# A scaled activation operand rebuilt from the parts of the raw one and a row of token factors, instead of from transposes

## The reference

```
h = rms_norm(x, norm_mix_w)
z = h @ w_in + b_in
```

```
y = xf * lax.rsqrt(jnp.mean(xf * xf, axis=-1, keepdims=True) + EPS)
return (y * g).astype(x.dtype)
```

## Time and profile before

| | |
|---|---|
| median of three runs | 1943.66 us |
| the profiled execution | 1943.68 us |
| its span | 1942.0 us |
| PE busy | 1928.6 us, 99% |
| DVE busy | 1380.6 us, 71% |
| ACT busy | 927.7 us, 48% |
| POOL busy | 237.3 us, 12% |

### The profile page before, as it was taken

How to read it: one execution, slowest core, us unless ns; L and a number is a source line. 1 busy time by engine, 2 the same in 40 slices (tenths; PEclk the granted TensorE clock), 3 DMA queues, 4 the chain that set the end, 5 groups by cost and what they waited for, 6 DMA issues and landing times.

```text
span 1942.0 us, 29945 instructions
## 1 busy us (share of the span) xinstructions
PE 1928.6 (99%) x11950; PEld 1723.7 (89%) x11950; DVE 1380.6 (71%) x1588; ACT 927.7 (48%) x1032; POOL 237.3 (12%) x195
## 2 busy tenths in 40 slices
PE   9999999999999999999999999999999999999998
PEld 7999888889998888888899998888888899998887
DVE  7776766668677666766769677667766769677666
ACT  6564444345645334544554445444544554445443
POOL 0000000000001000000049250000000049250000
PEclk9999999999999999999999999999999999999999
DMA  7544555554356554555444555555555454555553
GB/s 276 195 153 161 188 195 188 183 191 172 131 197 214 186 192 173 195 185 193 163 175 153 174 193 196 182 187 182 202 190 187 166 178 153 173 193 180 183 192 108
DMA packets 50738, 353.37 MB, mean 182 GB/s; under 512 B 6064, under 2 KB 6192, under 8 KB 9040
## 3 DMA queue, kind: packets, MB, share of 16 engines
q1 hardware_dynamic: 47952, 341.93, 50.1%
q0 software_dynamic: 2400, 9.99, 1.6%
q10 hardware_dynamic: 288, 0.05, 0.0%
HBM read 349.85 MB, written 2.10 MB: 181 GB/s over the span
## 4 chain that ended last, share of the span: by engine, by line
PE 90%; DVE 6%; ACT 2%; issue 1%; DMA 0%; DVEq 0%; POOL 0%; POOLq 0%; SPq 0%; ACTq 0%
PE ps L226 19%; PE ps L190 18%; PE ps L192 18%; PE ps L191 18%; PE ps L227 9%; PE ps L230 3%; DVE w_lo L166 2%; PE ps L229 1%; DVE conv_y L2124 1%; ACT w_hi L159 1%; PE ps L1287 1%; DVE score L2172 1%; ACT a L1668 0%; DVE top L2167 0%; PE ps L2305 0%
## 5 line engine op out<-in xcount | busy, mean ns | idle before, releaser
L166 DVE TENSOR_TENSOR w_lo<-raw,w_hi 128x2048 fp32r<-128x2048 f32 x317 | 734.5, 2320 | 277.2 <-ACT w_hi L159 276.2
L159 ACT ACTIVATE w_hi<-raw 128x2048 fp32r<-128x2048 f32 x317 | 606.5, 1916 | 402.4 <-PE ps L192 226.8
L226 PE MATMUL ps<-a,w_hi 128*128 128x512 f32 x1568 | 563.2, 398 | 2.3 <-DVE w_lo L166 1.3
L227 PE MATMUL ps<-a,w_lo 128*128 128x256 f32 x1568 | 440.5, 281 | 0.0
L226 PEld LDWEIGHTS ps<-a,w_hi 128*128 128x128 f32 x1568 | 295.3, 188 | 67.0 <-DVE w_lo L166 2.3
L190 PE MATMUL ps<-mixH,w_hi 128*128 128x256 f32 x1168 | 334.9, 287 | 0.2
L191 PE MATMUL ps<-mixL,w_hi 128*128 128x256 f32 x1168 | 330.9, 283 | 0.0
L192 PE MATMUL ps<-mixH,w_lo 128*128 128x256 f32 x1168 | 330.9, 283 | 0.0
L227 PEld LDWEIGHTS ps<-a,w_lo 128*128 128x128 f32 x1568 | 296.9, 189 | 8.9
L190 PE MATMUL ps<-w_hi,mixH 128*128 128x512 f32 x736 | 287.6, 391 | 0.0
L192 PE MATMUL ps<-w_hi,mixL 128*128 128x512 f32 x736 | 286.7, 390 | 0.0
(11 more groups left out here) (386 smaller groups left out, 2274.2 us busy)
## 6 DMA issues: line engine op xcount, KB each, us to landing
raw<-in_w_b SPq DMA_DIRECT2D x198, 1024.0 KB, 5.0
raw<-in_w_a SPq DMA_DIRECT2D x124, 1024.0 KB, 4.8
rows<-in_post_gains POOLq DMA_DIRECT2D x6, 512.0 KB, 4.2
rows<-in_rows_a POOLq DMA_DIRECT2D x2, 1028.0 KB, 7.3
raw<-in_w_a SPq DMA_DIRECT2D x4, 512.0 KB, 7.1
x<-in_x SPq DMA_DIRECT2D x2, 512.0 KB, 5.8
bias_line<-a_gates POOLq DMA_DIRECT2D x1, 1024.0 KB, 4.8
out<-x SPq DMA_DIRECT2D x4, 256.0 KB, 2.0
```

Of the source, the lines that this page charges most:

```text
L159: act.activation(k.w_hi[:, s, :], k.raw[:, s, :], ACT.Copy).then_inc(k.hi_ready, 1)
L166: dve.tensor_tensor(k.w_lo[:, s, :], k.raw[:, s, :], k.w_hi[:, s, :].bitcast(F32), ALU.subtract).then_inc(k.lo_ready, 1)
L226: pe.matmul(both, hi[:, kt, cols], k.a[:, :, kt, :], start=kt == 0, stop=False)
L227: pe.matmul(high, lo[:, kt, cols], k.a[:, 0, kt, :], start=False, stop=False)
```

## The change

The scaled operand is no longer made from x. In both kinds of layer POOL adds the first operand's high and low part (the feature gains are already in them) into `n_sum`; POOL also writes the 256 token factors as a row to device memory (`rstd_row`, element by element) and reads the row back to all 128 partitions as `rstd_all`. DVE multiplies `n_sum` by the row in four pieces of 128x512, ACT copies each piece to the high part, and DVE subtracts for the low part. The scalings of x and the 16 transposes of each layer are gone, and with them the PSUM reads. In the mixer PE takes the 16 small products before chunk M0+2 and waits for the scaled operand pair by pair in `feature(3)`; ACT and DVE split chunk M0+3 before they work on the operand; the load of `gain_row` stands behind the new transfers in POOL's list.

```
+def rstd_row(d, parts):
+    return bass.AP(tensor=d.bias_line.tensor, offset=3 * P, ap=[[1, P], [2 * SEQ, TT]] if parts is None
+                   else [[0, parts], [2 * SEQ, TT], [1, P]])
...
+            def spread_rstd(l):
+                pool.wait_ge(k.rstd_ready.sem, k.rstd_ready.at(l, 1))
+                pool.dma_start(rstd_row(d, None), k.rstd[:, 0:TT], allow_slow_non_contiguous=True).then_inc(row_stored.sem, 16)
+                pool.wait_ge(k.a_ready.sem, k.a_ready.at(l, 4))
+                for b in range(4):
+                    f = slice(2 * b, 2 * b + 2)
+                    pool.tensor_tensor(n_sum[:, f, :], k.aH[:, f, :].bitcast(F32), k.aL[:, f, :].bitcast(F32), ALU.add)\
+                        .then_inc(sums_ready.sem, 1)
+                pool.wait_ge(row_stored.sem, row_stored.at(l, 16))
+                pool.dma_start(rstd_all[:, :].rearrange("p (t n) -> p t n", t=TT), rstd_row(d, P)).then_inc(row_spread.sem, 16)
...
                     if n == 1:
-                        low_of(k, dve, l, 1, par[:, PA_NORM:PA_MLP], nH, nL)
+                        dve.wait_ge(row_spread.sem, row_spread.at(l, 16))
+                        for b in range(4):
+                            f = slice(2 * b, 2 * b + 2)
+                            dve.wait_ge(sums_ready.sem, sums_ready.at(l, b + 1))
+                            dve.tensor_tensor(n_sum[:, f, :], n_sum[:, f, :], mid(rstd_all[:, :], 2), ALU.mult).then_inc(n_made.sem, 1)
+                        for b in range(4):
+                            f = slice(2 * b, 2 * b + 2)
+                            dve.wait_ge(k.aH_ready.sem, k.aH_ready.at(l, 4 + b + 1))
+                            dve.tensor_tensor(nL[:, f, :], n_sum[:, f, :], nH[:, f, :].bitcast(F32), ALU.subtract)\
+                               .then_inc(k.a_ready.sem, 1)
                         low.upto(6)
...
+                def sum_parts(tt, parts):
+                    pool.wait_ge(x_ready.sem, x_ready.at(l, 8 + 4 * tt + parts[-1] + 1))
+                    f, n = slice(2 * parts[0], 2 * parts[-1] + 2), slice(tt * P, (tt + 1) * P)
+                    pool.tensor_tensor(n_sum[:, f, n], k.aH[:, f, n].bitcast(F32), k.aL[:, f, n].bitcast(F32), ALU.add)\
+                        .then_inc(sums_ready.sem, 1)
+
+                sum_parts(0, range(4))
+                sum_parts(1, range(2))
                 norm_root(l, 1)
+                pool.wait_ge(rstd_ready.sem, rstd_ready.at(l, 2))
+                pool.dma_start(rstd_row(d, None), rho, allow_slow_non_contiguous=True).then_inc(row_stored.sem, 16)
+                sum_parts(1, range(2, 4))
+                pool.wait_ge(row_stored.sem, row_stored.at(l, 16))
+                pool.dma_start(rstd_all.rearrange("p (t n) -> p t n", t=TT), rstd_row(d, P)).then_inc(row_spread.sem, 16)
                 pool.wait_ge(x_new.sem, x_new.at(l, 4))
                 pool.dma_start(gain_row[:, :], d.post_gains[l * 3 + 1].partition_broadcast(P)).then_inc(row_loaded.sem, 16)
...
-                low.upto(M0 + 2)
+                low.upto(M0 + 3)
...
+                dve.wait_ge(row_spread.sem, row_spread.at(l, 16))
+                n_full(0)
+                for b in range(3):
+                    n_full(b + 1)
+                    n_low(b)
+                n_low(3)
                 dve.tensor_tensor(ws, ws, mid(tri, 4), ALU.mult).then_inc(ch.sem, ch.one())
```

More of the change, by code:

```diff
@@ L282, in t_chunk @@
     ins.then_inc(k.chunk_done, 1)
[L285 to L290, removed]
 def split_high_half(k, act, st, layer, c, h):
@@ L363, in raw_transpose @@
         ins.then_inc(k.nT_done.sem, 1)
[L366 to L378, removed]
+def rstd_row(d, parts):
+    return bass.AP(tensor=d.bias_line.tensor, offset=3 * P, ap=[[1, P], [2 * SEQ, TT]] if parts is None
+                   else [[0, parts], [2 * SEQ, TT], [1, P]])
 def high_of(k, act, layer, stage, gain, dst, blocks=range(4)):
     for b in blocks:
-        act.wait_ge(k.nT_done.sem, k.nT_done.at(layer, 4 * stage + b + 1))
+        act.wait_ge(k.nT_done.sem, k.nT_done.at(layer, 4 * (stage // 2) + b + 1))
         for kk in range(2):
@@ L543, in _ @@
                     pool.wait_ge(line_ready.sem, 1)
-                    pool.dma_start(d.bias_line, line).then_inc(k.bias_moved, 16)
+                    pool.dma_start(d.bias_line[:, :, 0:3 * P], line[:, :, 0:3 * P]).then_inc(k.bias_moved, 16)
+                spread_rstd(l)
             pool.wait_ge(t_evicted.sem, t_evicted.at(DEPTH - 1, 4))
@@ L630, in _ @@
                     act.activation(cos[:, :, :], angle[:, 1], ACT.Sin).then_inc(trig_ready.sem, 1)
-                high_of(k, act, l, 1, par[:, PA_NORM:PA_MLP], nH)
+                for b in range(4):
+                    act.wait_ge(n_made.sem, n_made.at(l, b + 1))
+                    act.activation(nH[:, 2 * b:2 * b + 2, :], n_sum[:, 2 * b:2 * b + 2, :], ACT.Copy)\
+                       .then_inc(k.aH_ready.sem, 1)
                 act.wait_ge(half_ready.sem, half_ready.at(l, 1))
@@ L853, in _ @@
                 low.upto(3)
-                for h in range(2):
-                    cols = slice(h * DM // 2, (h + 1) * DM // 2)
-                    dve.tensor_scalar(k.xs[:, 1, cols], k.x[:, 1, cols], k.rstd[:, 1:2], None, ALU.mult)\
-                       .then_inc(k.scaled1.sem, 1)
                 dve.memset(z_pad[:, :, 0:CONV - 1], 0.0).then_inc(ch.sem, ch.one())
@@ L1773, in _ @@
                 norm_in(l, 1)
-                high.upto(M0 + 2)
+                high.upto(M0 + 3)
                 act.wait_ge(rstd_ready.sem, rstd_ready.at(l, 2))
-                for h in range(2):
-                    cols = slice(h * DM // 2, (h + 1) * DM // 2)
-                    act.activation(xs[:, 0, cols], k.x[:, 0, cols], ACT.Copy, scale=rho[:, 0:1]).then_inc(scaled0.sem, 1)
                 for tt in range(TT):
@@ L1786, in _ @@
                 for b in range(4):
-                    act.wait_ge(nT_done.sem, nT_done.at(l, b + 1))
-                    for kk in range(2):
-                        kt = 2 * b + kk
-                        ins = act.activation(nH[:, kt, :], k.ps[:, 4 + b, kk * SEQ:(kk + 1) * SEQ], ACT.Copy,
-                                             scale=norm_gain(1)[:, kt:kt + 1])
-                    ins.then_inc(nH_ready.sem, 1)
-                high.upto(M0 + 3)
+                    act.wait_ge(n_made.sem, n_made.at(l, b + 1))
+                    act.activation(nH[:, 2 * b:2 * b + 2, :], n_sum[:, 2 * b:2 * b + 2, :], ACT.Copy)\
+                       .then_inc(nH_ready.sem, 1)
                 act.wait_ge(gelu_ready.sem, gelu_ready.at(l, 2))
@@ L2463, in _, with n_pair @@
                 ins.then_inc(wi_done.sem, 1)
+                pe.wait_ge(k.lo_ready, st.count(l, M0 + 2))
+                t_chunk(k, pe, M0 + 2, range(8), 256, aop, lambda tt, h: k.ps[:, 0, tt * BW:(tt + 1) * BW], True, True)
+                def n_pair(i):
+                    pe.wait_ge(n_ready.sem, n_ready.at(l, i + 1))
                 def feature(i):
@@ L2473, in feature @@
                         pe.wait_ge(f_evicted.sem, f_evicted.at(l, i - 4))
-                    f_chunk(k, pe, M0 + i, [3 if i == 5 else i % 2], [range(8)], nop)
+                    f_chunk(k, pe, M0 + i, [3 if i == 5 else i % 2], [range(8)], nop, n_pair if i == 3 else None)
                 feature(3)
```

57 lines of the change are left out of this document (24 added, 33 removed).

## The result

| | |
|---|---|
| changed kernel, median of four runs | 1970.75 us (1967.42 to 1974.49) |
| kernel before, beside it | 1943.76 us (1943.62 to 1943.96) |
| ratio | 1.0139, 95% interval 1.0127 to 1.0151 |
| forecast | 1942.9 us, range 1938.5 to 1949.0 |

The change costs 27 us. The forecast was wrong in its likeliest case. Of the two rivals on the slow side, the late row had the right place, with a price (6 us over the forecast, where 27.8 was measured) that was between four and five times too small. The profiled execution is the shortest of the four, 1967.42 us with a span of 1965.7; before it was 1943.68 and 1942.0, so 23.7 us more have to be found in the trace.

A forecast was written before the change was run, and what follows sets the result against it. PE's own work was taken as the bound (busy 1928.6 of 1942.0 us). Transposes -6.8, held `post_add` +3.4, mixer row and operand +1.6, layer 0 +1.0 gave -0.8: 1942.9 us, range 1938.5 to 1949.0.

The forecast's parts named there:

- its likeliest case: Whole kernel: the forecast itself, 1942.9 us, own range 1940.5 to 1945.5, 49 in 100.
- the two rivals on the slow side: Mixers: row late, 1948.9 us, 20 in 100; row's issue held by VectorE's subtractions, 1947.2 us, 4 in 100.
- the late row: Mixers: store and row each take 4.8 us, operand starts at 979.2; 3.8 per mixer, 1948.9 us, 20 in 100.
- The transposes, -6.8.: PE, all four changed places: 16 transposes go at each, saving 1.7 us four times; called sure.
- `post_add` held, +3.4.: Mixers: POOL's 128x1024 addition holds VectorE's last two additions to x, costing PE 1.7 us per mixer.
- VectorE ready for the operand at 976.0.: First mixer: VectorE, held by POOL's last addition, ends the `w_lo` subtractions of M0+2 and M0+3 at 976.0.
- S + 2.0 to 5.2 and M0+4 at S + 11.2.: Mixers: pairs 2.0 to 5.2 us after VectorE starts the operand, M0+4 after 11.2; 0.8 per mixer, together +1.6.
- S = 976.0 to 976.5.: First mixer: VectorE starts the operand then, the store landing near 972 and the row at 974.5 to 976.5.
- `feature(3)` covered.: Mixers: PE takes the last pair at 982.0, ready by 981.7, so no wait there; covered by less than 1 us.
- Layer 0, +1.0.: First layer: chunk 6's `w_lo` ready at 45.5, PE waits about 1; 0 to 1.7 possible.
- The Trainium skill's rule on DVE and POOL's issues: Mixers: POOL's transfer issue waits during VectorE's two-SBUF-input operations; 2.1 more per mixer, 1947.2 us, 4 in 100.
- The range.: Whole kernel: 1938.5, leaving out most of the hidden-additions case, to 1949.0, including about half the late-row case.

The follow-up runs named there:

- one experiment: Changed kernel with the token-factor row made by PE, plus POOL's first two mixer additions waiting for VectorE's last piece of x: 1939.23 us, ratio 0.9973.
- row by PE, stores issued: Changed kernel with the token-factor row made by PE's products with ones, single-element stores still issued in all four places but unneeded: 1943.69 us, ratio 0.9998.
- no store: Changed kernel without the stores of the token factors, the row read from an input of the same shape instead: 1940.46 us, ratio 0.9984.
- the row by PE: Changed kernel with the row made by PE (diagonal tile times ones, read from PSUM) instead of through device memory: 1942.15 us, ratio 0.9993.

## Why the prediction was wrong, by its own steps

- *The transposes, -6.8.* Right: lines 376 and 2452 are gone, with 64 matmuls.
- *`post_add` held, +3.4.* Right: +3.1. The additions took 2.38 (I took 2.4), `post_add` 3.08 where 3.4 was forecast, and PE waited 1.3 per mixer before the transposes of x. Undone in one experiment, it gave 2.9 us.
- *VectorE ready for the operand at 976.0.* Right: 15.1 us after POOL's second root (974.92 - 959.82), where 14.9 was forecast. The two subtractions took 5.90 in place of some 4.5, held by POOL's last addition as worked out.
- *S + 2.0 to 5.2 and M0+4 at S + 11.2.* Right: the pairs at S + 2.1 to 5.3 in the changed kernel, and M0+4 within 0.03 us in nine profiles. What it costs PE when the row is in time was put a little high: with S 15.0 after the root (row by PE, stores issued) PE waits 0.47 and 0.45 before `feature(4)`, where 0.8 per mixer was taken.
- *S = 976.0 to 976.5.* This step failed. Its words: "I take 1.8 to 2.5 for each: the store lands near 972". The store took 11.6 and landed at 980, the row took 6.0. The 1.8 came from a load of 0.5 KB and the bound of 4.8 from loads of 128 KB; the trace of before has no store of single elements at all. I treated a bound from the nearest row as a bound on the operation, though that row was of another direction and another piece size. And "those of 128 KB at most 4.8" was not even right for that trace, whose DMA view has these lines as well:

```profile
bias<-bias_line POOLq DMA_DIRECT2D x4, 128.0 KB, 6.4
...
pos_i<-in_positions ACTq DMA_DIRECT2D x1, 1.0 KB, 4.6
```

The first is four loads of 128 KB on POOL's own queue (of eight issued in a row, among loads of weights), the second a load of two 4-byte numbers to each partition. With 4.6 for the store and 6.4 for the row the prediction's working gives S = 980.5, M0+4 at 991.7 and 1951.5 us (an estimate), already outside its range. The sum also has a slip: two transfers of 1.8 to 2.5 from 969.5 and 972 put the row at 973.8 to 974.5, not 974.5 to 976.5. The rival of the late row named "4-byte elements in the first and 1 MB weight loads around both" as its mechanism, and then priced it with the same 4.8. With the 11.6 and 6.0 measured in their place, its own working gives S = 987.1 on the clock of before, which is 985.8 on that of the changed kernel; 986.30 was measured.
- *`feature(3)` covered.* Wrong as a consequence, right where the row is in time (runs with no store, or with the row by PE).
- *Layer 0, +1.0.* +1.8 in the profile: DVE waited another 1.05 us for the row there, and without the store PE's wait is 0.5; where PE's wait grows to 2.8 the clock adds 1.7. When the row lands there was not worked out at all.
- *The Trainium skill's rule on DVE and POOL's issues ("SBUF — State Buffer", section "SBUF: two separate sides").* Rightly set aside, on thin ground: of the eight issues in the earlier trace rows only the first two start before the subtraction ends. In the changed kernel DVE stands idle at the row's issue (980.24) and until 969.02 at the store's (968.39), so these two do not try it. The run that does not wait for the store does: POOL issued two transfers from 969.95 on, in 0.58 and 0.54 us, while DVE's two subtractions ran until 974.38. (By the rule's own terms its price is 1946.9 to 1947.1, not 1947.2; nothing hangs on it.)
- *The range.* Its upper end, 1949.0, stood on the 4.8 us, which longer rows of the same trace contradict. An operation with no row of its kind in the trace wants an end that does not come from that trace's rows alone, or a chance for "many times the nearest row" as a case of its own.

## What to carry to other kernels

A small result that must be on all partitions soon should not go through device memory element by element: two products with ones on TensorE have a record of 0.60 us per place here, behind 0.5 to 1.6 us of VectorE for the diagonal tile, and the store alone took 8.3 to 11.6. If it must go through memory, turn it first so that each piece is 512 bytes, which halved the store. Before pricing a transfer, look for every row of the trace that is like it in size, piece and direction, and not only for the quickest. And where POOL is given work with two SBUF operands, start it behind VectorE's critical one: the same addition, 2 us later, gave 1.5 us in each mixer.

## What the runs showed of the hardware that was not expected

- A store of 256 elements of 4 bytes: 8.3 to 11.6 us to landing; of 128 elements: 7.9 to 8.7; of two pieces of 512 bytes: 4.4. What takes the time inside stays open. It is not the number of elements alone, nor POOL's queue, nor other traffic; whether it is the size of a piece, the 128 partitions they come from or the way of storing was not separated, since the run with two pieces changed them together.
- While such a store is under way, weight loads issued beside it move at 26 to 28 GB/s instead of some 250 (249 and 275 in the run without stores), and land after 11.5 us instead of 5.0.
- TensorE's granted clock: after an idle 1.8 us in layer 0 the products went on at 2.4 GHz, after 2.8 us at 1.2 GHz for 3.5 us, and after 9.7 us in the mixer the clock was 0.50 from 985 to 990 and 0.60 from 990 to 995. With useless products in the gap it stayed at 1.00. Whether that costs anything depends on who is the bound behind the gap: 1.7 us where PE was, 0.25 and nothing in the two mixers, where DVE's chain was.
- The four runs of the changed kernel lie 7 us apart and the ten without the store 0.6. The mean granted clock falls with the time (0.994 in the shortest, 0.990 in the longest), so part of the 27 us that the profile does not show, 3.3, is probably such gaps; that was not traced in a longer run.
